# Token selection redesigned, score matmuls alternated between array halves, and all low parts of the expert weights on VectorE

## The reference

```python
h = rms_norm(x, norm1_g) * (1 + sc1) + sh1            # sc, sh, g from silu(c) @ ada_w + ada_b
proj = h @ w_in
attn = windowed_gqa(q, k, v, attn_sink)               # 8 heads, 2 kv heads, head width 64
...                                                   # mLSTM branch, gates, output projection
x = x + g1 * (merged @ w_out)
h2 = rms_norm(x, norm2_g) * (1 + sc2) + sh2
x = x + g2 * hier_moe(h2, ...)
y = rms_norm(x, final_norm_g)

# hier_moe, t = 512 tokens, 4 groups of 4 experts
g_logits = t @ rg_w + rg_b;  grp = argmax(g_logits);  p_grp = softmax(g_logits)[grp]
e_logits = (t @ re_w + re_b)[group grp]
top_v, top_i = top_k(e_logits, 2);  top_w = softmax(top_v) * p_grp
out = sum over the two experts e of  top_w * ((silu(t @ w_gate[e]) * (t @ w_up[e])) @ w_down[e])
```

## Time and profile before

| what | value |
|---|---|
| median of three runs | 852.57 us (851.3 to 854.39) |
| the profiled execution | 853.12 us, of which the span from first to last instruction is 851.3 us |
| busy over the span | PE 741.4 us, PEld 595.2, DVE 513.2, ACT 384.9, POOL 415.7 |
| granted TensorE clock, mean | 0.937 of full |
| transfers | 196.31 MB, mean 231 GB/s |

### The profile page before, as it was taken

The page is one execution under the profiler, slowest core; times in us unless marked ns, Lnnn a source line. Parts: engine busy times, 40 slices in busy tenths (PEclk is TensorE's granted clock), DMA queues, the critical chain, the costliest instruction groups (busy, mean ns, idle before and its releaser), DMA issues.

```text
span 851.3 us, 10032 instructions
## 1 busy us (share of the span) xinstructions
PE 741.4 (87%) x3748; PEld 595.2 (70%) x3748; DVE 513.2 (60%) x641; ACT 384.9 (45%) x454; POOL 415.7 (49%) x167
## 2 busy tenths in 40 slices
PE   2889999989999999979997339999999999999920
PEld 1666777767888888868886337777778777787720
DVE  0435544350654456794237555888888878888827
ACT  3322222313425324423214226677767677777513
POOL 0422332333423223356731432878877887887740
PEclk9899999989999999999996559999999999999975
DMA  8949565447332232272318617999999999996353
GB/s 329 306 119 366 158 199 175 153 169 222 90 88 75 62 87 75 80 281 99 99 50 333 284 49 300 365 377 393 405 391 376 396 383 374 397 389 263 123 198 147
DMA packets 78026, 196.31 MB, mean 231 GB/s; under 512 B 13366, under 2 KB 46302, under 8 KB 71336
## 3 DMA queue, kind: packets, MB, share of 16 engines
q1 hardware_dynamic: 66368, 160.51, 52.1%
q0 software_dynamic: 5680, 21.81, 7.2%
q10 hardware_dynamic: 5944, 13.52, 4.3%
HBM read 179.00 MB, written 16.83 MB: 230 GB/s over the span
## 4 chain that ended last, share of the span: by engine, by line
PE 45%; POOL 19%; issue 11%; DVE 9%; POOLq 8%; DMA 4%; ACT 1%; SPq 1%; DVEq 0%; ACTq 0%
PE psum L723 31%; POOL up_low L2119 11%; POOLq L2138 8%; POOL down_low L2119 5%; PE psum L799 3%; DMA slots<-ada_w 2%; PE psum L781 2%; POOL inout L2114 2%; PE psum L948 2%; PE psum L715 2%; PE psum L893 1%; DMA front_ring<-w_in 1%; PE psum L928 1%; PE psum L809 1%; PE psum L907 1%
## 5 line engine op out<-in xcount | busy, mean ns | idle before, releaser
L2060 POOL TENSOR_TENSOR low_ring<-front_ring,high_ring 128x1024 fp32r<-128x1024 f32 x52 | 127.6, 2455 | 258.9 <-ACT high_ring L1176 258.9
L1176 ACT ACTIVATE high_ring<-front_ring 128x1024 fp32r<-128x1024 f32 x52 | 55.0, 1058 | 206.5 <-PE psum L723 143.1
L723 PE MATMUL psum<-chunk_high,xsT_low 128*128 128x512 f32 x264 | 107.3, 407 | 9.7 <-POOL up_low L2119 5.3
L1350 ACT ACTIVATE chunk_high<-front_ring 128x2048 fp32r<-128x2048 f32 x48 | 91.7, 1915 | 47.9 <-DVE inout L1968 24.3
L723 PE MATMUL psum<-h_low,high_ring 128*128 128x512 f32 x296 | 111.9, 396 | 0.0
L723 PE MATMUL psum<-chunk_high,xsT_high 128*128 128x512 f32 x264 | 104.0, 394 | 0.0
L2119 POOL TENSOR_TENSOR down_low<-front_ring,chunk_high 128x2048 fp32r<-128x2048 f32 x16 | 90.7, 5668 | 15.5 <-ACT chunk_high L1350 15.5
L723 PE MATMUL psum<-h_high,low_ring 128*128 128x512 f32 x232 | 94.9, 409 | 3.1 <-DVE h_low L1542 2.7
L723 PE MATMUL psum<-h_high,high_ring 128*128 128x512 f32 x232 | 91.2, 393 | 0.0
L1956 DVE TENSOR_TENSOR down_low<-front_ring,chunk_high 128x2048 fp32r<-128x2048 f32 x16 | 58.3, 3646 | 29.0 <-ACT chunk_high L1350 29.0
L1350 ACT ACTIVATE chunk_high<-slots 128x2048 fp32r<-128x2048 f32 x32 | 61.1, 1913 | 27.9 <-PE psum L1014 14.6
(11 more groups left out here) (294 smaller groups left out, 1557.3 us busy)
## 6 DMA issues: line engine op xcount, KB each, us to landing
front_ring<-w_down SPq DMA_DIRECT2D x16, 2048.0 KB, 11.5
front_ring<-w_in SPq DMA_DIRECT2D x34, 512.0 KB, 5.7
xbuf<-ada_w SPq DMA_DIRECT2D x32, 512.0 KB, 4.7
slot<-w_gate SPq DMA_DIRECT2D x8, 2048.0 KB, 11.4
slots<-w_up SPq DMA_DIRECT2D x8, 2048.0 KB, 10.5
slots<-w_gate SPq DMA_DIRECT2D x8, 2048.0 KB, 11.3
front_ring<-w_up SPq DMA_DIRECT2D x8, 2048.0 KB
y_rows<-inout ACTq DMA_DIRECT2D x16, 512.0 KB, 10.9
```

Of the source, the lines that this page charges most:

```text
L723: mm = pe.matmul(out, lhs(a, k), rhs(b, k), start=(start and k == 0 and a == 1), stop=(stop and k == count - 1 and (a, b) == (0, 0)))
L1176: act.activation(dst, src.rearrange("p (k n) -> p k n", k=KD), ACT.Copy).then_inc(high_ready, 1)
L1350: act.activation(chunk_high[place], raw_chunk(q, which, j), ACT.Copy).then_inc(chunk_split, 1)
L2060: pool.tensor_tensor(low, src, high.bitcast(F32), ALU.subtract).then_inc(low_ready, 1)
```

## The change

It has three parts.

- **Scores**: two heads of different kv heads alternate, matmul by matmul, each pair into two banks (n and n+2); VectorE empties the banks in the order 0, 2, 1, 3.
- **Selection**: the router is multiplied with x after the residual (`x1`), transposed before normalising, by weights scaled with `scale2`; a token's 1/rms and the constant shift times router weights come in afterwards, in the logits. The expert choice is a comparison of all four values of a group with each other. Tile lists are computed later, beside the first expert tile: loads of tiles 2 and 3, and gathers of 0 to 3, use fixed columns (`ids` becomes 64 wide, part j of an expert in columns 16j and up). h2 is made in steps: GpSimd multiplies with `scale2`, ScalarE with 1/rms, GpSimd adds the shift (three tiles; VectorE does the fourth). The first up load of tile 1 waits for h2; ScalarE's first up split waits for the stores.
- **Low parts**: GpSimd's two of each tile (`tile_lows`) go to VectorE (`second_part`); only two of tile 0 stay on GpSimd.

```diff
+SCORE_ORDER = (0, 2, 1, 3)
...
+LATE_BANKS = {"shiftw": 0, "shiftwb": 1, "router0": 0, "router1": 1, "logits0": 2, "logits1": 3, "rank": 4,
+              "ids": 5, "counts": 7}
+LATE_BANKS |= {f"wo{t}.{h}": t + 4 * (1 - h) for t in range(TT) for h in range(2)}
+LATE_BANKS |= {f"x1T{t}.{h}": 4 + t for t in range(TT) for h in range(2)}
...
@@ TensorE, scores @@
-                for n in range(A_HEADS // 2):
-                    name = f"score{b}.{n}"
-                    wait_bank(pe, name)
-                    for h in (2 * n, 2 * n + 1):
-                        at, j = h // PAIRS * A_HD, h % PAIRS
...
+                for n in range(2):
+                    names = [f"score{b}.{n}", f"score{b}.{n + 2}"]
+                    for name in names:
+                        wait_bank(pe, name)
+                    for i in range(2):
+                        for kv, name in enumerate(names):
+                            j = 2 * n + i
+                            mm = pe.matmul(bank(name)[:, i * SEQ:(i + 1) * SEQ],
+                                           rot[kv * A_HD:(kv + 1) * A_HD, 1 + j, b * P:(b + 1) * P],
+                                           rot[kv * A_HD:(kv + 1) * A_HD, 0, r * SEQ:(r + 1) * SEQ],
+                                           start=True, stop=True)
...
@@ TensorE, output product and router @@
+            def router_shift():
+                wait_bank(pe, "shiftw")
+                pe.wait_ge(router_landed, 16 * 2)
+                product("shiftw", bank("shiftw", 20)[0:REQS, :], lambda k: modT[:, 6 + k // 4, k % 4, :],
+                        lambda k: router_w[:, k, :], KD)
...
+            def route_half(r, h):
+                for g in range(4):
+                    mm = pe.matmul(bank(f"router{r}")[g * QUAD:(g + 1) * QUAD, 0:SEQ], scaled_w[:, r, 4 * h + g, :],
+                                   x1T[:, 4 * h + g, r * SEQ:(r + 1) * SEQ], start=(h == 0), stop=(h == 1))
...
+            router_shift()
+            for j in range(4):
+                pe.wait_ge(merged_ready, 2 * j + 2)
+                tokens_out(("wo0", j), [f"wo{t}.0" for t in range(TT)], merged)
+                if j == 0:
+                    spread_shift()
+            for j in range(4):
+                if j == 3:
+                    for t in range(TT):
+                        turn_x1(t, 0)
+                tokens_out(("wo1", j), [f"wo{t}.1" for t in range(TT)], merged)
+            turn_x1(0, 1)
+            turn_x1(1, 1)
...
@@ SP @@
             load_in(1, 1, 0)
+            load_down(0, 0)
+            sp.wait_ge(h2_pool, TT - 1)
+            sp.wait_ge(h2_dve, 1)
             load_in(1, 1, 1)
-            load_down(0, 0)
...
@@ ScalarE @@
+            act.wait_ge(rstd_ready, 1)
+            for t in range(TT - 1):
+                act.wait_ge(u_ready, TT + t + 1)
+                act.activation(u_rows[:, t, :], u_rows[:, t, :], ACT.Copy, scale=rstd[:, t:t + 1]).then_inc(v_ready, 1)
...
-            wait_full(act, "ids")
+            act.wait_ge(h2_stored, 16 * TT)
             act.wait_ge(moe_landed[1], 16)
             split_chunk(0, 1, 0, 2)
+            wait_full(act, "ids")
             split_chunk(0, 1, 1, 3)
...
@@ VectorE, selection (its start; rank, places and ids follow) @@
+            link(dve.tensor_tensor(beaten, quads.rearrange("p q (i j) -> p q i j", i=1).to_broadcast([P, n_quads, 4, 4]),
+                                   quads.rearrange("p q (i j) -> p q i j", j=1).to_broadcast([P, n_quads, 4, 4]),
+                                   ALU.is_gt))
...
+            dve.tensor_reduce(losses, beaten, AX.X, ALU.add)
+            link(dve.tensor_reduce(wins, beaten.rearrange("p q i j -> p q j i"), AX.X, ALU.add))
+            link(dve.tensor_tensor(losses, losses, wins, ALU.subtract))
...
@@ VectorE, expert tiles @@
+            def second_part(q, which, place):
+                dve.tensor_tensor(low_chunk(q, which, 1), raw_chunk(q, which, 1), chunk_high[place].bitcast(F32),
+                                  ALU.subtract).then_inc(second_low, 1)
...
                     empty_y(q)
+                dve.wait_ge(chunk_split, 6 * s + 2)
+                second_part(q, 1, (place + 3) % RING)
                 dve.wait_ge(heT_high, s)
                 split_he(heT)
...
                 gated(q)
+                dve.wait_ge(chunk_split, 6 * s + 4)
+                second_part(1 - q, 2, 3 - 2 * q)
...
@@ GpSimd @@
             wait_full(pool, "upa7")
+            pool.wait_ge(hm_ready, TT)
...
+            for h in range(2):
+                for t in range(TT):
+                    half = slice(h * COLS, (h + 1) * COLS)
+                    wait_emptied(pool, f"wo{t}.{h}")
+                    pool.tensor_tensor(u_rows[:, t, half], xbuf[:, t, half], scale2[:, t // TPR, half], ALU.mult
+                                       ).then_inc(u_ready, 1)
...
+            for t in range(TT - 1):
+                pool.wait_ge(v_ready, t + 1)
+                pool.tensor_tensor(h2[:, t, :], u_rows[:, t, :], shift2[:, t // TPR, :], ALU.add).then_inc(h2_pool, 1)
+                pool.wait_ge(h2_pool, t + 1)
+                store_h2(t)
+            pool.wait_ge(h2_dve, 1)
+            store_h2(TT - 1)
...
-            def tile_lows(s, q, place):
...
```

More of the change, by code:

```diff
@@ new lines, in spread_shift, with turn_x1 @@
+            def spread_shift():
+                wait_bank(pe, "shiftwb")
+                wait_emptied(pe, "shiftw")
+                for r in range(REQS):
+                    mm = pe.matmul(bank("shiftwb")[:, r * 20:(r + 1) * 20],
+                                   ident[0:REQS, r:r + 1].to_broadcast([REQS, P]), shift_w, start=True, stop=True)
+                mm.then_inc(psum_full, 1)
+            def turn_x1(t, h):
+                wait_emptied(pe, f"wo{t}.{h}")
+                transposes(f"x1T{t}.{h}", [xbuf[:, t, (4 * h + n) * P:(4 * h + n + 1) * P] for n in range(4)])
@@ L1799, in _ @@
-            logits = route[:, 0:80].rearrange("p (t n) -> p t n", t=TT)
-            for t in range(TT):
-                wait_full(dve, f"logit{t}")
-                emptied(dve.tensor_tensor(logits[:, t, :], bank(f"logit{t}", 20), router_b[:, :], ALU.add))
-            wait_emptied(dve, "logit3")
-            dve.wait_ge(late_landed, 16)
-            def three(a, w, n=4):
-                return route[:, a:a + w].rearrange("p (t n) -> p t n", n=n)
-            def over(ap, n=4):
-                return ap.rearrange("p (t a) -> p t a", a=1).to_broadcast([P, TT, n])
@@ L1945, in _ @@
-            wait_full(dve, "ids")
-            emptied(dve.tensor_copy(ids[:, :], bank("ids", 2 * MAX_PAIRS)))
+            for t in range(2, TT):
+                wait_full(dve, f"x1T{t}.1")
+                emptied(dve.tensor_copy(x1T[:, 4:8, t * P:(t + 1) * P],
+                                        bank(f"x1T{t}.1").rearrange("p (k t) -> p k t", t=P)))
+            for r in range(REQS):
+                wait_full(dve, f"router{r}")
+                emptied(dve.tensor_copy(router_parts[:, r * SEQ:(r + 1) * SEQ], bank(f"router{r}", SEQ)))
@@ new lines, in _ @@
+            by_tile = logits.rearrange("p (t n) -> p t n", t=TT)
+            g_log, e_log = by_tile[:, :, 0:N_GRP], by_tile[:, :, N_GRP:20]
+            over = lambda a: a.rearrange("p (t a) -> p t a", a=1).to_broadcast([P, TT, 4])
+            for n, value in enumerate((best, second)):
+                link(dve.tensor_tensor(prod[:, n], c12[:, n], e_log, ALU.mult))
+                link(dve.tensor_reduce(value, prod[:, n], AX.X, ALU.add))
+            dve.tensor_tensor(gate_terms[:, 16:20], second, best, ALU.subtract)
```

542 lines of the change are left out of this document (308 added, 234 removed).

## The result

The changed kernel takes **829.0 us** (median, 827.6 to 830.01), the kernel before 853.21 in the same measurement: ratio 0.9717, 95% interval 0.9693 to 0.9741. The change gains 24.2 us. I had forecast 34.5 us and 818 us, so the sign was right and the size was wrong: 829.0 lies at the upper edge of the range (809 to 829).

What follows compares the result with a forecast made beforehand. TensorE was taken to bound most of the kernel (45% of the chain), with GpSimd and its queue at 27%. Gains of 5.0 + 15.3 + 1.3 + 12.6 + 0.3 = 34.5 us off 853.12 gave 818 us, range 809 to 829.

Steps and rivals of the forecast that it cites:

- part 3: Token selection between output product and experts: gather at 485, first expert matmul at 493.4, 15.3 us earlier than before.
- Half the old landing time puts it at 485: Selection: the h2 stores, the last issued at 476, land in half their old 16.5 us, so the gather starts at 485.
- rival C: Selection: GpSimd's adds take all 7.2 us, stores land as slowly as before; first matmul only 8 us earlier, 825; chance 0.13.
- The stores, not the ids, are late next: Selection: the gather waits for the h2 stores, in at 485, rather than for the ids, ready at 481.
- Scores: Attention stage: alternating array halves overlap, each block's run of 16 matmuls falls from 2.90 to 1.65 us, gaining 5.0 us.
- Item 2: TensorE before selection: added shift product, its 2.6 us idle, and transposes start selection 6.2 us later (bounds 3 and 8).
- Steady tiles: Expert stage: with all low parts on VectorE the tile period falls from 18.87 to 17.9 us, gaining 12.6 us over 13 tiles.
- Rival F: Expert stage: VectorE becomes the bound with a tile of 24.2 us, making the kernel slower, about 900; chance 0.03.
- rival B: Expert stage: transfers set the time, 18.4 us a tile, 7 us less gain, 825; chance 0.15.
- item 4: Expert stage, all low parts on VectorE: TensorE becomes the bound, 12.6 us gained; at 408.7 GB/s transfers, 11.5.
- The end: Kernel's end: two GpSimd waits of 0.5 us go, TensorE's wait for the y copy grows by 0.6; gain 0.3 us.

Runs made afterwards that it cites:

- best: Changed kernel with second up, first down and final-gain loads behind the first two gathers, tail_shift's reorderings, and all h2 rows made by VectorE: 814.5 us, ratio 0.9528.
- hold_up1: Changed kernel with the second up load (2 MB) and the final gain's load (0.5 MB) waiting until the h2 rows are stored: 826.64 us, ratio 0.9665.
- hold_gather_dve: Changed kernel with second up, first down and final-gain loads behind the first two gathers, and VectorE making tile 0's up low parts: 822.31 us, ratio 0.9616.
- tail_shift: Changed kernel with VectorE's y copy ahead of the last low part, and the shift product behind the output product's first piece: 821.32 us, ratio 0.9621.
- lows_gpsimd: Changed kernel with only its third part undone, so GpSimd again makes two of a tile's six low parts: 843.41 us, ratio 0.9866.
- hold_two: Changed kernel with second up, first down and final-gain loads held, the up and down loads until the h2 rows are stored: 827.92 us, ratio 0.9678.

## Why the prediction was right and wrong

**The step that failed most** is in part 3: "Half the old landing time puts it at 485." In the frame of that sum E was 455.9; in the trace it is 451.2, so 4.7 us are to be added to the times of the trace. Then the last store is issued at 475.0 (forecast 476) and the ids are ready at 480.6 (481), but the stores are in at 490.3 (485.56 + 4.7) and not 485, and the first expert matmul is at 499.2 and not 493.4. The landing took 15.3 us, not 9. I had argued that the loads in flight beside it were nearly in by then. They were not, and the load that I called held behind the last store is held only until h2 is made: it was issued at 469.76, 0.5 us ahead of that store. So 8.4 MB from 452 on, with 2.1 MB of stores, one more load of 2.1 MB and 0.5 MB of gains released beside the last store, make 13.1 MB, and at some 420 GB/s those need 31 us, to 483. The sum of bytes up to the last store was there to be made, and would have given the landing to within 3 us. This is half of rival C, "stores land as slowly as now"; its other half, that GpSimd's additions take all 7.2 us, didn't happen (I charged 6, and the issue time came within 1 us).

Windows of the changed kernel from the first loads to 483, and of best (8.4 MB in all) before and during its last store's landing:

```profile
453.00:483.00 30.00, 8.75 (x58) 7.01 (x54) 25.60 (x55) 11.86 (x14) 12.13 (x10) 0.63 0.99 415
...
449.00:467.00 18.00, 6.40 (x45) 4.77 (x44) 16.68 (x45) 7.37 (x10) 4.04 (x6) 0.66 0.99 400
467.00:471.80 4.80, 2.11 (x11) 2.00 (x10) 3.63 (x7) 1.03 (x2) 0.00 (x0) 0.50 0.49 200
```

hold_up1 shows the mechanism: take 2.5 MB away and the landing falls from 15.3 to about 9 us. The sum of bytes is a lower bound, though. It gives E + 32, E + 26 and E + 21 for the changed kernel, hold_up1 and best, and the stores were in at E + 34.4, E + 28.0 and about E + 25: when the pile is gone, the last stores move at 200 GB/s. I had also written "The stores, not the ids, are late next", which was right, and left it at one link. Behind the stores stood the gather, which loses to released loads, and behind that VectorE, held by GpSimd. With these freed (hold_gather_dve) the first expert matmul comes 6 to 8 us sooner than in the two traces of the changed kernel, which is the missing 5.5 us and a little more.

**Scores**, forecast 5.0, got 2.2, mis-sized twice. The overlap takes a run from 2.90 to 1.93 us and not to 1.65: 3.9 us in four blocks instead of 5.0. And 1.6 us more went in the first block, which ran partly at the lower clock level (3.28 us instead of 2.0, and 1.49 behind it instead of 1.13), while the trace of before has it at full clock. By the Trainium skill's up to 2x (TensorEngine Tiling (Array Packing), Theoretical Speedup) the term was 5.8. The trace shows a factor of 1.5 for fp32 with 64 rows.

**Item 2**, forecast -6.2: the idle before the shift product is 2.44 us (forecast 2.6). First score matmul to E grew by 3.7 us (236.56 to 240.29) although the scores gained 2.2, so item 2 cost 5.9 between these two traces (up to 7.5 by the other traces with the same work, 240.3 to 241.9). Right, and tail_shift shows that 1.9 to 2.4 of it could be had back.

**Steady tiles**, forecast 17.9 us and 12.6 in all, got 17.96 and 11.8. Right: VectorE's low parts have a mean of 2.28, TensorE never waits in them, and lows_gpsimd shows that part 3 alone does it. A row of the changed kernel's page:

```profile
L2093 DVE TENSOR_TENSOR down_low<-front_ring,chunk_high 128x2048 fp32r<-128x2048 f32 x16 | 36.5, 2284 | 0.0
```

Rival F (VectorE the bound) is refuted by the same rows, and so is rival B: ScalarE's chunk splits never wait for a load in the whole stage, only for VectorE and TensorE. Transfers move 408 to 419 GB/s, where I took 404 as full. A slip in item 4: 13 x 0.9 is 11.7, not 11.5.

**The end**, forecast +0.3, got -1.5. I had the wait for the y copy at 1.07 + 0.6; it is 2.72, and I had not foreseen that TensorE's clock falls behind such a wait, which costs another 1.4 us. tail_shift shows both.

## What to carry to other kernels

When a transfer is on the critical path, add up all bytes that are issued before it lands and divide by the rate that the trace shows: here its landing time was that of the whole pile, 2 to 4 us more, and not its own. Prefetches that nobody needs yet belong behind it, and behind the next small transfer too, or the wait only moves. Where several waits stand in a row, a fix of one can measure as nothing; read the trace up to the next releaser before giving it up, and expect gains to appear only when the last link is out.

## What was not expected of the hardware

- The granted clock of TensorE falls from 1.00 to about 0.5 behind a wait of 2.7 us in an otherwise busy stretch (779 to 785 us), and doesn't fall behind one of 1.07 us. Ahead of the first score block stand two waits of 0.9 and 0.35 us with short matmuls between, in every trace. In 12 of the 14 traces of this study the clock fell there and stayed low for 3 to 10 us of full work; in that of the kernel before and in best it didn't. What decides it is open.
- The same gather of 128 rows reached TensorE in 4.5 us with little else in flight, 9.1 beside one load of 2 MB released with it, and 12.6 beside two.
- GpSimd's issue of a gather took 1.02 us with VectorE idle, and 2.24 and then 1.84 us beside VectorE's low parts of the gate (478.20 in hold_two). The Trainium skill (SBUF — State Buffer, SBUF: two separate sides) tells of GpSimd being kept from writing descriptors while VectorE runs an instruction in a 2-port mode. It doesn't say so of the two-input subtractions that stood beside these gathers; the trace shows about 1 us a gather there, and which port they met on is open.
